# A three-block transformer: the delta gates' small steps in another order, and other PSUM banks for the keys' norm sums

## The reference

```
proj = x @ w_in                       # split into qkv, z, a, b, uv, gate_dn, gate_sgu
qkv  = silu(causal_depthwise_conv(qkv, conv_w))
q = l2_normalize(q) * 128 ** -0.5;  k = l2_normalize(k)          # 8 heads of 128
beta = sigmoid(b)
g = -exp(a_log) * softplus(a + dt_bias)                          # 256 tokens x 8 heads
g_cum = cumsum(g) in chunks of 64;  decay = exp(g_cum[t] - g_cum[s])
o = gated delta rule(q, k, v, g, beta)                           # chunked, triangular inverse
```

## Time and profile before

| | |
|---|---|
| median of 3 runs | 1308.7 us (1306.21 to 1308.98) |
| the profiled execution | 1311.17 us, span 1309.4 us |
| tensor engine, matmuls | 1265.4 us busy, 97% of the span |
| VectorE | 832.6 us, 64% |
| ScalarE | 600.5 us, 46% |
| GpSimd | 170.2 us, 13% |
| mean granted clock of the tensor engine | 0.987 |

### The profile page before, as it was taken

The page is one execution under the profiler, slowest core; times in us unless marked ns, Lnnn a source line. Parts: engine busy times, 40 slices in busy tenths (PEclk is TensorE's granted clock), DMA queues, the critical chain, the costliest instruction groups (busy, mean ns, idle before and its releaser), DMA issues.

```text
span 1309.4 us, 20713 instructions
## 1 busy us (share of the span) xinstructions
PE 1265.4 (97%) x8950; PEld 1180.4 (90%) x8950; DVE 832.6 (64%) x980; ACT 600.5 (46%) x697; POOL 170.2 (13%) x132
## 2 busy tenths in 40 slices
PE   7999999999999999999899999899999999999996
PEld 7977999998998899998889999899998999999995
DVE  6566865557655775556699448863776765555554
ACT  4464533335645533333575346624833543333331
POOL 8400400001300040000402200120000050000002
PEclk9999999999999999999989999999999999999999
DMA  9712575554643475558786447563764465555550
GB/s 269 172 65 97 165 238 182 189 192 122 201 161 97 132 255 181 181 187 142 129 143 101 97 91 126 110 107 55 225 206 162 139 204 180 187 192 191 180 176 33
DMA packets 160220, 205.02 MB, mean 157 GB/s; under 512 B 13571, under 2 KB 142322, under 8 KB 160130
## 3 DMA queue, kind: packets, MB, share of 16 engines
q1 hardware_dynamic: 157906, 195.80, 53.6%
q0 software_dynamic: 2224, 7.90, 2.0%
HBM read 202.63 MB, written 1.05 MB: 156 GB/s over the span
## 4 chain that ended last, share of the span: by engine, by line
PE 88%; DVE 5%; ACT 4%; DMA 2%; issue 1%; POOLq 0%; POOL 0%; DVEq 0%; ACTq 0%
PE PS L366 25%; PE PS L367 24%; PE PS L368 24%; DMA ring<-in_w_in 2%; DVE w_lo L1020 2%; PE PS L869 1%; PE PS L853 1%; PE PS L865 1%; PE PS L516 1%; ACT AR L1633 1%; ACT w_hi L1603 1%; PE PS L594 1%; PE PS L616 1%; PE PS L765 1%; PE PS L771 1%
## 5 line engine op out<-in xcount | busy, mean ns | idle before, releaser
L1020 DVE TENSOR_TENSOR w_lo<-ring,w_hi 128x2048 fp32r<-128x2048 f32 x182 | 434.7, 2392 | 207.1 <-ACT w_hi L1603 206.7
L366 PE MATMUL PS<-x_hi,w_hi 128*128 128x256 f32 x1648 | 477.2, 290 | 2.6 <-DVE w_lo L1115 2.1
L368 PE MATMUL PS<-x_hi,w_lo 128*128 128x256 f32 x1648 | 468.5, 284 | 0.0
L367 PE MATMUL PS<-x_lo,w_hi 128*128 128x256 f32 x1648 | 468.4, 284 | 0.0
L1603 ACT ACTIVATE w_hi<-ring 128x2048 fp32r<-128x2048 f32 x182 | 347.3, 1912 | 241.7 <-PE PS L368 229.2
L366 PEld LDWEIGHTS PS<-x_hi,w_hi 128*128 128x128 f32 x1648 | 318.6, 193 | 8.5 <-issue 3.4
L367 PEld LDWEIGHTS PS<-x_lo,w_hi 128*128 128x128 f32 x1648 | 318.4, 193 | 3.9 <-issue 2.2
L368 PEld LDWEIGHTS PS<-x_hi,w_lo 128*128 128x128 f32 x1648 | 318.0, 193 | 0.0
L1615 ACT ACTIVATE AR<-PS 128x512 f32<-128x512 f32 (+1 forms) x144 | 82.1, 586 | 306.5 <-PE PS L368 187.7
L366 PE MATMUL PS<-w_hi,o_hi 128*128 128x512 f32 x480 | 188.5, 393 | 1.3 <-ACT res L1615 0.8
L367 PE MATMUL PS<-w_lo,o_hi 128*128 128x512 f32 x480 | 187.4, 390 | 0.0
(11 more groups left out here) (370 smaller groups left out, 1341.4 us busy)
## 6 DMA issues: line engine op xcount, KB each, us to landing
ring<-in_mlp_w SPq DMA_DIRECT2D x64, 1024.0 KB, 5.3
ring<-in_w_in SPq DMA_DIRECT2D x32, 1024.0 KB, 11.5
ring<-in_expert_w_gate SPq DMA_DIRECT2D x16, 1024.0 KB, 5.4
ring<-in_expert_w_up SPq DMA_DIRECT2D x16, 1024.0 KB, 5.4
ring<-in_expert_w_down SPq DMA_DIRECT2D x16, 1024.0 KB, 4.9
ring<-in_c_w_in SPq DMA_DIRECT2D x12, 1024.0 KB, 5.5
ring<-in_a_w_in SPq DMA_DIRECT2D x4, 1024.0 KB, 8.6
ring<-in_c_w_out SPq DMA_DIRECT2D x4, 1024.0 KB, 5.0
```

The source lines that it names most:

```text
L366: mm(out, a_hi, b_hi, start=first, stop=False, skip_group_check=True)
L367: mm(out, a_hi, b_lo, start=False, stop=False, skip_group_check=True)
L368: return mm(out, a_lo, b_hi, start=False, stop=last, skip_group_check=True)
L1020: v.tensor_tensor(w_lo[:, m % PARTS], ring[:, index[split[m]] % RING], w_hi[:, m % PARTS].bitcast(F32), ALU.subtract)\
```

## The change

Three things change. On the tensor engine, `turn[0]` goes up by two ahead of the keys' norm sums, in both halves. On VectorE, the copies of `abT` and `ab` ask for no piece ahead, and the piece beyond `ab` is split behind the bias addition. On ScalarE, the exponential of `a_log` moves ahead of the wait, beta's exponential ahead of the logarithm, the logarithm gives the signal, and one exponential of a constant follows it.

```diff
@@ tensor engine, for hb in range(2)
                 advance(fill, 6)
+                turn[0] += 2
                 for j in (2, 3):
                     norm_sums("qn", hb, j, 4, "qk_squares", 6)
                 advance(fill, 20)
@@ VectorE
             v.memset(s_raw[:, :, :, 0:3], 0.0).then_inc(S("raw_pad"), 1)
-            ps = bank("abT", 1)
+            ps = bank("abT", 0)
             evacuated(v.tensor_copy(s_abT[0:16], ps[0:16, 0:T]), "abT")
-            ps = bank("ab", 1)
+            ps = bank("ab", 0)
             evacuated(v.tensor_copy(s_ab[:], ps[:, 0:64].rearrange("p (t c) -> p t c", t=TT)[:, :, 0:16]), "ab")
-            read("ab", 1)
+            read("ab", 0)
             v.tensor_tensor(y_, s_ab[:, :, 0:8], adt[:, 1:2].broadcast_to([P, TT, 8]), ALU.add).then_inc(S("ab_ready"), 1)
+            split_ahead(pieces_for["ab"], 1)
             ve.wait_ge(S("ab_act"), 1)
@@ ScalarE
             raw(0, 0)
             split_ahead(pieces_for["ab"], 1)
+            a(adt[:, 0], adt[:, 0], ACT.Exp)
             act.wait_ge(S("ab_ready"), 1)
             after(a(f_kb, y_, ACT.Abs))
-            after(a(f_kb, f_kb, ACT.Exp, scale=-1.0))
-            a(f_kb, f_kb, ACT.Ln, bias=1.0)
-            a(adt[:, 0], adt[:, 0], ACT.Exp)
-            a(beta, s_ab[:, :, 8:16], ACT.Exp, scale=-1.0).then_inc(S("ab_act"), 1)
+            ins = a(f_kb, f_kb, ACT.Exp, scale=-1.0)
+            a(beta, s_ab[:, :, 8:16], ACT.Exp, scale=-1.0)
+            after(ins)
+            a(f_kb, f_kb, ACT.Ln, bias=1.0).then_inc(S("ab_act"), 1)
+            a(cst[:, 3:4], cst[:, 0:1], ACT.Exp)
             split_ahead(pieces_for["gc"])
```

## The result

The changed kernel took 1312.67 us, median of 14 runs (1310.41 to 1315.49), against 1308.7 for the kernel before (14 runs, 1306.21 to 1313.29): 1.003 times as long, 95% interval 1.0021 to 1.004. It is 4.0 us slower. Forecast were 1306.4 us and, as the range, 1302.8 to 1311.0. The profiled execution took 1311.8 us (span 1310.0, mean granted clock 0.987); the one before, 1311.17 (span 1309.4).

What follows compares the result with a forecast made beforehand. The tensor engine, busy 97% of the span, was taken as the bound, its waits and low clock costing 12.6 us. First half -0.1, banks -1.9, uv0 -0.8, low clock +0.5: -2.3, so 1306.4 us; range 1302.8 to 1311.0.

Steps and rivals of the forecast that it cites:

- the landing of v0's load: Weight load in the first half: issued at 646.3 instead of 639.13, landing at 655.8 to 661.8, taken as 658.
- q1's low half: Made behind the first copy, not at 634.6: tensor engine waits 2.85 us at q1, low clock costs 1.3 more.
- The gates: ScalarE's signal at 650.9, gates 651.05 to 651.65; the 2.2 us wait at line 796 and 3.4 us of clock go.
- From landing to convolution: First half: the first convolution starts 5.0 us after v0's load lands, at 663.0 instead of 660.60.
- The head products of the first half: They start at 695.0 against 695.17, so -0.1 us; by the bounds of the landing -2.0 to +3.7.
- The banks, second half: The 3.28 us wait goes, a 1.5 us one comes; head products -3.2 us, of which 1.9 is kept.
- uv0: Weight piece that moves off the bank of uv7 to one emptied long ago: its wait goes, -0.8 us.
- yg3's bank: Taken by the output product's second bank: slack 0.5 us, so no cost; at worst 1.8 us.
- -0.1 + 0.5: First half's head products -0.1 us, and 0.5 us added for what low clock costs in the first half.
- the slower rival: v0's late load blocks ScalarE and the convolution chain; landing at 663 with both clock spells +3.5, 1312 us; chance 0.18.
- second spell of low clock: First half, in the tensor engine's wait ahead of the squares: would add up to 1.2 us.
- v0 lands early: Rival: landing by 656.5, first half gains 1.5 to 2 us, in all -4.5, 1304.2 us; chance 0.25.

Runs made afterwards that it cites:

- e8: The kernel before, unchanged, profiled a second time to see which clock spells and waits repeat: one execution, 1306.56 us.
- e3: The changed kernel with `bank("abT", 1)` for `bank("abT", 0)`, so q1's low half is made early as before the change: 1304.03 us, ratio 0.9969.
- e4: The kernel before with only ScalarE's part of the change: 1310.0 us, ratio 1.0007.

## Why the prediction was wrong

The first step that failed is one term: the landing of v0's load. "By bounds it lands at 655.8 to 661.8; I take 658, since over half of the shorter time is spent alone", with the issue at 646.3. The last product of `abT` starts 1.18 us earlier in the profile after than in the one before, so the times of the profile after are raised by that much for the comparison; before, then after:

```profile
643.33 0.28 PE L368 MATMUL PS<-x_hi,n_lo 128*128 128x256 f32 x1
```
```profile
642.15 0.28 PE L368 MATMUL PS<-x_hi,n_lo 128*128 128x256 f32 x1
```

In that count the load was issued at 646.4 and landed at 661.4. I had read the 15.5 us of the earlier trace rows as 9.5 made longer by company. They were the place in the weight, and two rows could not tell the one from the other. Nor had k1's 9.5 us been those of a load alone: v0's was issued 4.4 us behind it. All 32 pieces of that trace would have raised the doubt: k0, v0, z0 and uv0 took 15.5, 15.5, 15.3 and 14.5 us, and 15 of the others under 11.

- *q1's low half.* Right: 2.85 us, the lower end; then the low clock for 3.4 us. In it the products begin every 0.21 us instead of every 0.12, so 1.5 are lost (taken 1.3). By that measure the forecast's 3.4 and 1.7 us for the spells of the profile before are 3.0 and 1.5.
- *The gates.* Right in the main: the wait at line 796 and its low clock are gone. ScalarE's signal came at 652.3 in the count of the profile before, forecast 650.9, since q1's first triples and the transposes ran at the low clock; the tensor engine did not wait for it even so. The bias addition took 0.17 us where it had taken 2.16 beside GpSimd; now GpSimd is done at 643.1, as the row below shows, and it is q1's low half that starts beside it and takes 2.42 us. The rule of the Trainium skill that the two engines lock each other out (SBUF — State Buffer, "two separate sides") agrees: with no instruction of GpSimd beside it, the addition is short.

```profile
640.70 2.37 POOL L2057 TENSOR_TENSOR xt<-xt,gb 128x1024 f32<-128x1024 f32 x1
```

- *From landing to convolution.* Right: 665.29 - 660.24 = 5.05 us, forecast 5.0. With the landing at 661.4 this gives 666.5 against 663.0.
- *The head products of the first half.* Forecast -0.1, measured +4.8 (698.81 + 1.18 - 695.17). 3.4 us are the landing. Another 1.2 are ScalarE's: it was to gain the 0.84 us for which it had waited for the tensor engine, and it waits 1.22 instead (687.93, against the earlier trace rows), as that engine had lost 4.84 us ahead of the squares and more to the low clock behind them. That spell had been named as a possibility, up to 1.2 us.
- *The banks, second half.* -3.2 forecast for the head products; -3.1 measured (835.04 + 1.18 - 834.49 = +1.7, after +4.8), with the new wait of 1.33 (forecast 1.5) and the clock full. Of the 3.1 the inverse gives 1.0 back: the products at line 917 (918 in the changed kernel) stand at +2.7 (908.62 + 1.18 - 907.05). So 2.1 are kept, and 1.9 was forecast. VectorE's first update of the inverse comes 3.9 us later than in the earlier trace rows, with no wait for the tensor engine ahead of it, as it would if VectorE is what comes last there; no run tests that.
- *uv0.* Right: the wait is gone, and from +2.7 ahead of it the count falls to +1.7 at the norm sums behind it (916.16 + 1.18 - 915.60), 1.0 against a forecast of 0.8.

Before, then after:

```profile
907.05 0.33 PE L917 MATMUL PS<-AR 128*128 128x64 f32 x2
...
915.60 1.88 PE L765 MATMUL PS<-AR,ones 128*128 128x512 f32 x4
```
```profile
852.88 2.47 DVE L1430 TENSOR_TENSOR AR<-AR,PS 128x512 f32<-128x512 f32 x4
...
908.62 0.33 PE L918 MATMUL PS<-AR 128*128 128x64 f32 x2
...
916.16 1.88 PE L765 MATMUL PS<-AR,ones 128*128 128x512 f32 x4
```

- *yg3's bank.* Right, no wait.

Together +1.8 us in the two profiles (4.8 - 2.1 - 1.0 + 0.1), and +4.0 in the medians. So the second half and uv0 came out as forecast, and the whole miss is in the first half. The profile before was a long one: it had spells of low clock near 440 us (granted clock 0.86 from 436 to 448, 1.00 in the one after), behind the wait of 3.28 us, and near 1017. In a second profile of the unchanged kernel (e8) that wait was 2.8 us, the clock stayed full at all three places, and the execution took 1306.56.

> The kernel before, profiled a second time, to see which of its clock spells and of the waits of the stage repeat. My theory: the waits (2.2, 1.2 and 3.28 us) repeat to 0.1 us; the spells of low clock move by a few us and their number changes by one or two, 1.7 us each; that is why the two profiled executions lie nearer to each other (1311.2 and 1311.8 us) than the medians (1308.8 and 1312.7). Rival: clock spells and all repeat exactly.

The waits of 2.2 and 1.2 us repeated to 0.1 us, as expected; that of 3.28 did not.

So the forecast against 1308.7 started from a profile 2.5 us over the median, and the one after was 0.9 under its own; a sum of that kind can't be closed better than by some 2 us. The parts, timed, are clearer: banks -2.7 or -3.6 (the forecast's -1.9 and -0.8 are -2.7), gates +6.6 to +7.6 where -0.1 + 0.5 was forecast.

What happened is the slower rival as it was written: the late load, ScalarE blocked, the convolution chain behind it; "it decides from a landing of 660.5 with a second spell of low clock". It landed at 661.4, with the spell. Its price was set at 1312, and 1312.67 was measured. Its chance of 0.18 was too small. The landing was put between two bounds by how long each company lasted, when the only observation of that very piece was the upper one; and the rival "v0 lands early" got 0.25 on the strength of another piece's load.

## What to carry to other kernels

A call that asks for "no piece ahead" moves more than a low half: it moves the slot that this frees, so the next load, so every engine that stands in order behind that load; follow a moved step down to the first engine that blocks on it. Take the time of a load from its own earlier row, and look whether loads of one tensor fall into two groups before putting a long one down to traffic. Where a piece's place makes it slow, change the order so that it is issued with time to spare: that, with the low half back in its place, made this change a gain of 7 us.

## What had not been expected of the hardware

- A load of the same size, shape and place in the order takes about 9 us or about 15, by the column at which it begins: 14.3, 15.0 and 15.2 us from 4096, 8192 and 0 bytes into the row, 8.6, 8.9 and 9.0 from 11264, 10240 and 9216. The DMA engines were as busy from 8192 as from 10240 (1.03 and 1.00), at 77 and 214 GB/s.
- The clock after a wait isn't a matter of its length alone. It stayed full after 1.2 and 1.33 us, after 2.23 (e3) and 2.58 (e4) ahead of the squares, and after 2.8 in the second profile of the kernel before. It was low after 1.91 in the very trace of e4, after 2.2 (line 796) and 2.85 (q1), for 6.8 and 3.4 us, and after 3.28.
